# Weight products moved beside four waiting places of a two-block transformer kernel on one Trainium2 core

## The chip, the core and the metric

The program runs on one NeuronCore of one Trainium2 chip. The number that counts is the device time of one execution in microseconds (us). Three executions of the kernel before took 2319.35, 2320.1 and 2322.78 us, the median being 2320.1.

## The reference, cut to what matters

Two transformer blocks run one after the other over x of 512 tokens by 1024 features, in float32. The first has three attention branches and a feed-forward part; the change does not touch it. The second, which the change is about, computes:

```
h = rmsnorm_2(x, norm_mix)
qa, ka, va, za, alpha, beta, qb, kb, vb, ga, gb = _split_cols(h @ w_in, IN_SPLITS)
qa, ka, va = silu(_causal_dwconv(concat(qa, ka, va), conv_w))
g = -exp(a_log) * softplus(alpha + dt_bias); beta = sigmoid(beta); G = cumsum(g) in each chunk of 64
oa = _gated_deltanet(qa, ka, va, alpha, beta, a_log, dt_bias)       # 8 heads of 128
oa = rmsnorm_2(oa, head_norm) * silu(za)
ob = _chunk_band_attention(qb, kb, vb, band_bias)                   # 16 heads of 64, softmax
y = sigmoid(ga) * (oa @ w_a_out) + sigmoid(gb) * (ob @ w_b_out)
x = x + y @ w_o
q = rmsnorm_2(x, norm_xattn) @ w_mq;  kk, vv = split(rmsnorm_2(mem, norm_mem) @ w_mkv)
x = x + (softmax(q kk^T / 16) vv) @ w_mo                            # 4 heads of 256, 256 memory tokens
gate, up = split(rmsnorm_2(x, norm_ffn) @ w_gate_up)
x = x + (silu(gate) * up) @ w_down
```

## The kernel before

Everything is kept transposed, features on the 128 partitions and the 512 tokens along the free dimension. **A product** is 128 output columns of one weight matrix: eight weight blocks of 128x128 for an input of 1024 features. To reach float32 accuracy in the fast fp32r format each operand is split in a high and a low part, and each block takes three matmuls of 128x512: high by high (L1034), low by high (L1036), high by low (L1040). So a product is 24 matmuls. Key and value products of the memory (`mem_kv`) have 256 tokens and matmuls of 128x256. All small products (scores, sums, probabilities by v) go through `mm` at L989, all turnings (transposes by TensorE) through `tr` at L992.

**The weights** come in units of eight blocks (128x1024 float32, 512 KB), packed in the order in which the products use them. SyncE loads unit i+2 into one of three stage buffers (L2430), ScalarE copies unit i+1 to fp32r as whi (L1477), and VectorE (L1855) or GpSimd, here POOL (L2331), subtracts to get wlo. In the gated delta rule and the branch product behind it POOL does this, later VectorE. This step, `feed`, stands ahead of every eighth block in the order of work of all engines.

**The order of work** is written by class `Schedule`. Generators yield steps of one place in the program each; a step of a product is two blocks, six matmuls. `mix` alternates between generators, `par` merges them in proportion to their lengths, `pipe` chains products so that what follows one (a turning, say) stands some steps into the next, and an empty step (`repeat([], n)`) leaves n turns to the others. `settle` then makes one list, and every engine works through its part of it in that order and never passes a step that waits. It also gives each step its PSUM bank. Products alternate between b0 and b1 by a counter `gi`, which counts every product, and turnings marked "spare" take whichever of the two the counter says is free:

```
            if kind == "mm" and what[1] == 0:
                gi += 1
...
                if place == "gemm":
                    place = f"b{gi % 2}"
                elif place == "spare":
                    place = f"b{(gi if ended else gi + 1) % 2}"
```

A `Use` of a place carries in `freed` the events after which the next user may write to it; for a turning that is `act_turn`, ScalarE's copy out of the bank.

The four places that the change touches, in order of time:

1. `gdn_scalars` (L688) runs beside the first projections of the gated delta rule's first head (`mix` in `block2`). The product for alpha and beta, w_in_2 4096, is scaled by VectorE into tile ya; `gs_in` turns it (bank<-cft,ya), ScalarE and VectorE make g (tile al) and beta (tile be); `gs_cols` sums g in the chunks (bank<-al,cft), from which ScalarE takes gcol and VectorE ercol; `gs_rows` makes the same sums as rows (bank<-cft,al and cft,be). The rr in the scaling is the norm's factor, from the matmuls bank<-acc,cft.
2. `gated("a2")` (L589) is the branch oa @ w_a_out. Its first products begin in `opened` (L610): steps k0 to k5, which read the first six heads' output, before the last two heads are needed. oah and oal are the high and low part of the last head's output.
3. The band stage in `block2` (L802 on): `soft_pair` works through a couple of heads in four blocks of 128 queries (`sm_s` scores, `sm_max`, `sm_exp`, `sm_turn` the turning bank<-cft,bdp of the probabilities, copied by ScalarE to bdpt, `sm_pv` bank<-bdpt,bv). Beside couple p run the q, k and v products of couple p+1, and `raw_gate` products for the later branch as listed in `beside`. The v product (tile bvT) is turned (bank<-cft,bvT) and copied by ScalarE to bv (L1556); the o copies are obh.
4. `xattn`: after `mem_kv` with its 16 products, `cross(i, j)` works on memory head i in two halves, each with scores (bank<-mk,xq), exponential (xap, L1663), turning and the product with mv. The q products of head i+2 (`proj`) stand beside heads 0 and 1.

Of the kernel before, what the change touches and what calls it, by code (L numbers as in the profile page):

```python
# [293 lines left out]
def st(kind, what, *uses):  # L294
    return kind, what, uses
# [7 lines left out]
def mix(*parts):  # L303
    parts = list(parts)
    while parts:
        for p in list(parts):
            if (s := next(p, None)) is None:
                parts.remove(p)
            else:
                yield s  # L310
# [11 lines left out]
def par(*parts):  # L322
    parts = [list(p) for p in parts]
    done = [0] * len(parts)
    while any(n < len(p) for n, p in zip(done, parts)):
        i = min((i for i in range(len(parts)) if done[i] < len(parts[i])), key=lambda i: (done[i] + 0.5) / len(parts[i]))
        yield parts[i][done[i]]
        done[i] += 1
# [43 lines left out]
class Schedule:  # L372
# [15 lines left out]

    def raw_gate(self, name, col, out, ph):

        return self.gemm(name, col, range(8), ("H", ph), "h", None, [("dve_ev", (name, col, 0))], extra=[Use(f"raw{col}", [])], out=out)

    def gate(self, name, col, out, place, ph):
        return self.gemm(name, col, range(8), ("H", ph), "gate", place, [("dve_ev", (name, col, 0))], out=out)
# [194 lines left out]
    def gated(self, tag, ph, gates, branches, bufs, pre, late=False):  # L589
        n, mg = 0, {"b1": "mg1", "b2": "mg2"}.get(tag)  # L590
        if tag == "a2":
            yield from self.opened(tag, branches, bufs, pre)
        for m in range(2 if tag == "a2" else 0, 8):
            A = bufs[2 + m % 2]
            uA = Use(f"{tag}acc{m % 2}", [("gt_copy", m)] if tag == "a2" else [("sp_hi", (mg, m)), ("sp_lo", (mg, m))])
            for j, ((gname, gcol), (bname, src, nk)) in enumerate(zip(gates, branches)):
                gkey, bkey = (gname, gcol + 128 * m, 0), (bname, 128 * m, 0)
                s, t_ = pre.get((m, j), (bufs[n % 2], f"{tag}s{n % 2}"))[0], bufs[4 + n % 2]
                if late and (m, j) in pre:
                    yield [st("late_gate", (gkey, s))]  # L600
                if (m, j) not in pre:
                    yield from self.gate(gname, gcol + 128 * m, s, Use(f"{tag}s{n % 2}", [("dve_ev", bkey)]), ph)
                ut = Use(f"{tag}t{n % 2}", [("gt_add", (tag, m, j))])
                yield from self.gemm(bname, 128 * m, range(nk), src, "branch", uA if j == 0 else ut, [("dve_ev", bkey)],
                                     s=s, A=A, t=t_, j=j, tag=tag, m=m, s_key=gkey)
                n += 1
            ref = ("gt_add", (tag, m, len(gates) - 1)) if len(gates) > 1 else ("dve_ev", bkey)
            yield [st("merge", (tag, m, A, ref))]

    def opened(self, tag, branches, bufs, pre):  # L610

        (bname, src, nk), made = branches[0], []
        for m in range(2):
            A, bkey = bufs[2 + m], (bname, 128 * m, 0)
            g = self.gemm(bname, 128 * m, range(nk), src, "branch", Use(f"{tag}acc{m}", [("gt_copy", m)]), [("dve_ev", bkey)],
                          s=pre[m, 0][0], A=A, t=None, j=0, tag=tag, m=m, s_key=("w_in_2", 7184 + 128 * m, 0))
            made.append((g, [st("merge", (tag, m, A, ("dve_ev", bkey)))]))
        for g, _ in made:
            yield from islice(g, nk // 2 - 1)
        for g, merge in made:  # L620
            yield from g
            yield merge
# [64 lines left out]

    def gdn_scalars(self):  # L688
        u = Use("b5", [("gs_be", 0)])
        yield [st("gs_in", u, u)]  # L690
        yield from repeat([], 5)
        u = Use("b7", [("gs_er", 0)])
        yield [st("gs_cols", u, u)]
        ub, ub2 = Use("b7", [("gs_row", 0)]), Use("b6", [("gs_row", 1)])
        rows = [Use(f"gbc{h}", self.gbc_freed(h)) for h in range(2)]
        yield [st("gs_rows", (ub, ub2), ub, ub2)]
        yield from repeat([], 8)
        yield [st("gs_store", None)] + [st("gdn_rows", (h, rows[h]), rows[h]) for h in range(2)]
# [108 lines left out]
    def block2(self):  # L807
        k = self.k
        yield [st("lo_engine", "pool"), st("gdn_start", None)]
        yield from self.proj("w_in_2", 4096, k.goT, Use("goT", [("pe_small", "gdn")]), "mix2")  # L810
        yield from mix(self.gdn_scalars(), self.gdn_proj(0))
        pre = {}

        def pre_gates(i):
            bufs = [(f"g{n}{i}", k.g3[i][n]) for n in "qkv"] + ([("gz2", k.gz[2]), ("gz0", k.gz[0])] if i else [])
            for m, (place, b) in enumerate(bufs, 3 * i):
                pre[m, 0] = b[:], place
                yield from self.gate("w_in_2", 7184 + 128 * m, b[:], Use(place, []), "mix2")
        yield [st("none", None, *(Use(n, [("st_rows", 0)]) for n in ("gD", "gL")))]
        yield [self.decay(0, "chunk", ("gp_lt", 0))]  # L820
        for h in range(9):
            g = []
            if h >= 1:
                g.append(self.gdn_scan(h - 1))
            if h < 8:
                g.append(self.gdn_prep(h))
                g.append(self.gdn_proj(h + 1))
            if h >= 7:
                g.append(pre_gates(h - 7))
            yield from par(*g)  # L830
        yield [st("fence", "a2")]
        yield from self.gated("a2", "mix2", [("w_in_2", 7184)], [("w_a_out_2", "oa", 8)], k.a2buf, pre)
        yield [st("fence", "band"), st("lo_engine", "dve"), st("tables", None), st("load_mem", 2)]

        def proj(p):
            s, d = p % 2, self.done2("band", p)
            return [(self.proj("w_in_2", 4112 + 128 * p, k.bq[s][:], Use(f"bq{s}", d), "mix2", scale=0.125), None),
                    (self.proj("w_in_2", 5136 + 128 * p, k.bk[s][:], Use(f"bk{s}", d), "mix2"), None),
                    self.values("w_in_2", 6160 + 128 * p, "mix2", k.bvT, "bvT", k.bv[s], Use(f"bv{s}", d))]

        early = {}

        def gates(*ms):
            for m in ms:
                early[m, 0] = k.bgate[m][:], None
            return [(self.raw_gate("w_in_2", 8208 + 128 * m, k.bgate[m][:], "mix2"), None) for m in ms]
        beside = [[], [], [], gates(0), gates(1), gates(2), gates(3), gates(4, 5)]

        def band_loads(p):
            for h in (2 * p, 2 * p + 1):  # L850
                u = Use(f"band{h % 4}", [("sm_mx", (("band", h // 2, h % 2), 3))])
                yield [st("band_load", (h, u), u)]
        yield from band_loads(0)
        yield from pipe(proj(0))
        for p in range(8):
            if p < 7:
                yield from band_loads(p + 1)
            yield from par(self.soft_pair("band", p, "bd", "ob"), pipe((proj(p + 1) if p < 7 else []) + beside[p]))
        yield [st("fence", "mg2")]
        yield from self.gated("b2", "mix2", [("w_in_2", 8208)], [("w_b_out_2", "ob", 8)], k.b2buf, early, True)  # L860
        yield from self.residual("w_o_2", "mg2", range(8), "x2", "norm_xattn_2", ("w_in_2", 8208 + 896, 0))
        yield [st("fence", "xattn")]
# [25 lines left out]
    def xattn(self):  # L888
        k = self.k
        yield [st("tables", None)]  # L890

        def proj(i):
            for j in range(2):
                s = 2 * (i % 3) + j
                yield from self.proj("w_mq_2", 256 * i + 128 * j, k.xq[s][:], Use(f"xq{s}", [("pe_xo", (i, 1)), ("pe_xo", (i, 3))]), "x2")
        yield from par(seq(proj(0), proj(1)), self.mem_norm(2, "norm_mem_2"))
        yield from self.mem_kv(2, "w_mkv_2", k.raw2, 8, k.mk2, k.mv2, None, range(16))
        self.xo = [[Use(f"b{6 + j}", [("o_hi", ("o3", 2 * i + j)), ("o_lo", ("o3", 2 * i + j))]) for j in range(2)] for i in range(4)]
        for i in range(4):
            yield from par(self.cross(i, 0), self.cross(i, 1), *([proj(i + 2)] if i < 2 else []))  # L900
            yield [st("xa_out", i)]
        yield from self.residual("w_mo_2", "o3", range(8), "ffn", "norm_ffn_2", ("w_mq_2", 896, 0))
        yield [st("fence", "ff2")]
# [1677 lines left out]
```

How the kernel before makes its waits and increments, by code:

```python
    def free(use):  # L994
        for ref in use.before:
            if fresh(*ref):
                pe.wait_ge(*at(*ref))
# [1 line left out]
    def wait(*refs):  # L999
        for ref in refs:
            if fresh(*ref):
                pe.wait_ge(*at(*ref))
# [19 lines left out]
    def product(g, x):  # L1022
        o = bank[g.use.bank][:, 0:g.n]
        if x == 0:
            free(g.use)
        for j in (x, x + 1):
            unit, n = divmod(g.blocks[j], UNIT)
            c = slice(128 * n, 128 * n + 128)
            wh, wl = k.whi[unit % NSPLIT][:, c], k.wlo[unit % NSPLIT][:, c]
            hi, lo, hi_refs, lo_refs = moving(g, g.ks[j])
            if fresh("whi", unit):
                pe.wait_ge(*at("whi", unit))
            wait(*hi_refs)
            pe.matmul(o, wh, hi, start=j == 0, stop=False)
            wait(*lo_refs)
            pe.matmul(o, wh, lo, start=False, stop=False)
            if fresh(k.lo_sem[unit], unit):
                pe.wait_ge(*at(k.lo_sem[unit], unit))
            end = j == len(g.ks) - 1
            i = pe.matmul(o, wl, hi, start=False, stop=end)
            if end or n == UNIT - 1 or g.blocks[j] == len(k.blocks) - 1:
                i.then_inc(*up("pe_w", *([("unit", unit)] if n == UNIT - 1 else []), *([g.key] if end else [])))
# [1 line left out]
    def rms(ph, use):  # L1044
        if ph == "mix":
            pe.wait_ge(*at("ld_cf", 0))
        if ph == "fin":
            pe.wait_ge(*at("acc_add", (ph, 6)))
            free(use)
# [13 lines left out]
    def head_norm(o):  # L1063
        pe.wait_ge(*at("hn_sq", o.no))
        free(o.u_bank)
```

## Time and profile before

| | |
|---|---|
| median of three executions | 2320.1 us |
| their range | 2319.35 to 2322.78 us |
| the profiled execution, in all | 2320.8 us |
| its span, first to last instruction | 2319.0 us |
| TensorE (PE) busy, 13098 matmuls | 2254.3 us, 97% |
| TensorE weight loads (PEld) | 1798.2 us, 78% |
| VectorE (DVE) busy | 1141.5 us, 49% |
| ScalarE (ACT) busy | 892.9 us, 39% |
| GpSimd (POOL) busy | 443.7 us, 19% |
| mean DMA rate | 86 GB/s |

The page comes from one execution recorded by the hardware profiler. A row of the timeline gives start, duration, engine, line, operation, tiles (out<-in) and, in brackets, how long the engine had been idle and what ended that. The ends of matmuls are modelled and overlap the next start. Equal neighbours are drawn together in one row (x4). The granted clock is TensorE's, as a share of full speed.

### The profile page before, as it was taken

How to read it: one execution, taken by the hardware profiler on the slowest of the kernel's cores; microseconds unless marked ns; L12 is line 12 of the kernel's file. 1: busy time of each engine (PE TensorE's matmuls, PEld its weight loads, DVE VectorE, ACT ScalarE, POOL GpSimd, SP SyncE). 2: the span in 40 equal slices, each digit the busy share in tenths (PEclk: the TensorE clock that was granted, in tenths of full speed). 3: DMA queues.
4: the chain of work that ended last, by engine and by line, in shares of the span. 5: the costliest groups of instructions: out<-in, count | busy, mean ns of one | idle time of the engine just before them, and what ended most of it. 6: DMA issues, size and time to landing. Idle time of an engine off the chain costs nothing.

```text
span 2319.0 us, 32779 instructions
## 1 busy us (share of the span) xinstructions
PE 2254.3 (97%) x13098; PEld 1798.2 (78%) x13098; DVE 1141.5 (49%) x1949; ACT 892.9 (39%) x1427; POOL 443.7 (19%) x300
## 2 busy tenths in 40 slices
PE   8999999999999999999999999999999999999998
PEld 6776777888888888777777777777788988888886
DVE  4433454444544445575666512555546445435444
ACT  5544564233322223434443442444434434222223
POOL 2332221001201102444353332000011001101001
PEclk9999999999999999999999999999999999999999
DMA  4223212323333233221121123222232513233322
GB/s 166 73 64 101 64 46 82 100 92 99 93 98 101 92 99 92 95 71 47 47 70 51 38 66 128 81 82 83 63 100 92 155 37 100 91 100 100 98 93 82
DMA packets 58358, 198.95 MB, mean 86 GB/s; under 512 B 6736, under 2 KB 6864, under 8 KB 57952
## 3 DMA queue, kind: packets, MB, share of 16 engines
q1 hardware_dynamic: 58208, 196.86, 27.0%
q8 instruction: 105, 1.72, 0.3%
q14 instruction: 45, 0.37, 0.1%
HBM read 194.67 MB, written 2.16 MB: 85 GB/s over the span
## 4 chain that ended last, share of the span: by engine, by line
PE 87%; DVE 6%; ACT 3%; issue 2%; DMA 1%; POOL 0%; SPq 0%; DVEq 0%; ACTq 0%; POOLq 0%
PE bank L1034 24%; PE bank L1040 24%; PE bank L1036 24%; PE bank L989 13%; PE bank L992 2%; ACT whi L1477 1%; DMA stage<-in_wall 1%; DVE ya L1855 1%; DVE gk L1858 1%; DVE wlo L1855 0%; DVE gk L2130 0%; DVE sbA L2032 0%; SPq L2430 0%; DVE gq L1858 0%; DVE gv L1858 0%
## 5 line engine op out<-in xcount | busy, mean ns | idle before, releaser
L1034 PE MATMUL bank<-hh,whi 128*128 128x512 f32 x1680 | 688.0, 410 | 1.1 <-ACT nm1r L1517 0.6
L1040 PE MATMUL bank<-hh,wlo 128*128 128x512 f32 x1680 | 658.1, 392 | 4.8 <-DVE wlo L1855 3.1
L1036 PE MATMUL bank<-hl,whi 128*128 128x512 f32 x1680 | 656.0, 390 | 0.0
L1477 ACT ACTIVATE whi<-stage 128x1024 fp32r<-128x1024 f32 x340 | 357.3, 1051 | 326.5 <-PE bank L1040 315.5
L1855 DVE TENSOR_TENSOR wlo<-stage,whi 128x1024 fp32r<-128x1024 f32 x252 | 331.5, 1316 | 295.6 <-ACT whi L1477 295.1
L1040 PEld LDWEIGHTS bank<-hh,wlo 128*128 128x128 f32 x1680 | 315.9, 188 | 75.9 <-DVE wlo L1855 5.7
L1034 PEld LDWEIGHTS bank<-hh,whi 128*128 128x128 f32 x1680 | 316.5, 188 | 73.2 <-issue 9.3
L1036 PEld LDWEIGHTS bank<-hl,whi 128*128 128x128 f32 x1680 | 316.8, 189 | 63.6 <-issue 5.3
L2331 POOL TENSOR_TENSOR wlo<-stage,whi 128x1024 fp32r<-128x1024 f32 x88 | 210.6, 2393 | 408.1 <-ACT whi L1477 408.1
L1855 DVE TENSOR_TENSOR x<-bank,x 128x512 f32<-128x512 f32 x80 | 55.3, 691 | 152.6 <-PE bank L1040 152.6
L2331 POOL TENSOR_TENSOR acc<-acc,sqb 128x512 f32<-128x512 f32 x34 | 45.2, 1329 | 288.9 <-ACT sqb L1490 288.9
L1034 PE MATMUL bank<-u1h,whi 128*128 128x512 f32 x256 | 99.6, 389 | 0.0
L1036 PE MATMUL bank<-u1l,whi 128*128 128x512 f32 x256 | 99.6, 389 | 0.0
L1040 PE MATMUL bank<-u1h,wlo 128*128 128x512 f32 x256 | 99.6, 389 | 0.0
L2331 POOL TENSOR_TENSOR u1l<-f1t,u1h 128x512 fp32r<-128x512 f32 x32 | 41.3, 1292 | 265.2 <-ACT u1h L1575 265.2
L2331 POOL TENSOR_TENSOR u2l<-f2s,u2h 128x512 fp32r<-128x512 f32 x22 | 28.4, 1293 | 299.7 <-ACT u2h L1584 299.7
L989 PEld LDWEIGHTS bank<-ya 64*64 64x64 f32 (+1 forms) x2048 | 58.9, 138 | 32.2 <-issue 16.5
L989 PE MATMUL bank<-ya 64*64 64x64 f32 (+2 forms) x2048 | 72.4, 231 | 5.9 <-DVE ya L1855 5.8
L1575 ACT ACTIVATE u1h<-f1t 128x512 fp32r<-128x512 f32 x32 | 20.2, 632 | 126.6 <-DVE f1t L1855 126.6
L1036 PE MATMUL bank<-u2l,whi 128*128 128x512 f32 x176 | 68.6, 390 | 0.0
L1034 PE MATMUL bank<-u2h,whi 128*128 128x512 f32 x176 | 68.5, 389 | 0.0
L1040 PE MATMUL bank<-u2h,wlo 128*128 128x512 f32 x176 | 68.5, 389 | 0.0
(374 smaller groups left out, 3446.4 us busy)
## 6 DMA issues: line engine op xcount, KB each, us to landing
stage<-in_wall SPq DMA_DIRECT2D x340, 512.0 KB, 3.6
band<-in_toep SPq DMA_DIRECT2D x16, 256.0 KB, 3.9
x<-in_xT SPq DMA_DIRECT2D x8, 256.0 KB, 5.2
fb<-rowsf SPq DMA_DIRECT2D x8, 256.0 KB, 3.7
gbc<-rows SPq DMA_DIRECT2D x8, 256.0 KB, 3.3
gbc<-rowsc SPq DMA_DIRECT2D x16, 128.0 KB, 3.6
out_y<-fout SPq DMA_DIRECT2D x8, 256.0 KB, 2.3
memx<-in_memT SPq DMA_DIRECT2D x1, 1024.0 KB, 10.0
```

The source lines that it names most:

```text
L989: return pe.matmul(out, w, r, start=start, stop=stop, skip_group_check=True)
L992: return pe.transpose(out, in_, k.cf("ident"))
L1034: pe.matmul(o, wh, hi, start=j == 0, stop=False)
L1036: pe.matmul(o, wh, lo, start=False, stop=False)
L1040: i = pe.matmul(o, wl, hi, start=False, stop=end)
L1477: act.activation(k.whi[u % NSPLIT][:], k.stage[u % NSTAGE][:], ACT.Copy).then_inc(*up("whi", u))
L1575: act.activation(k.u1[0][:, a["t"] % 16, :], a["b"][:], ACT.Copy).then_inc(*up("sp_hi", ("u1", a["t"])))
L1855: return dve.tensor_tensor(out, a, b, op)
L1858: return dve.scalar_tensor_tensor(out=out, in0=a, scalar=s, in1=b, op0=op0, op1=op1)
L2331: return pool.tensor_tensor(out, a, b, op)
```

## The change

It does four things. `gdn_scalars` lets three steps of others go by before `gs_in`. `opened` begins four products, each in a bank of its own from b2 to b5, instead of two, and the loop of `gated` goes on at the fifth. In the band stage the raw gates are in bank b7 and run as one stream, three steps beside each of couples 0 to 6 and the rest, nine, beside couple 7; before, they stood whole beside couples 3 to 6 with two beside 7. In `xattn` the last four key and value products stand beside cross attention's head 0, and the q products of heads 2 and 3 move on to stand beside heads 1 and 2; head 3 has none.

```diff
--- before.py
+++ after.py
@@ -388,7 +388,8 @@
 
     def raw_gate(self, name, col, out, ph):
 
-        return self.gemm(name, col, range(8), ("H", ph), "h", None, [("dve_ev", (name, col, 0))], extra=[Use(f"raw{col}", [])], out=out)
+        return self.gemm(name, col, range(8), ("H", ph), "h", None, [("dve_ev", (name, col, 0))], extra=[Use(f"raw{col}", [])],
+                         bank="b7", out=out)
 
     def gate(self, name, col, out, place, ph):
         return self.gemm(name, col, range(8), ("H", ph), "gate", place, [("dve_ev", (name, col, 0))], out=out)
@@ -590,7 +591,7 @@
         n, mg = 0, {"b1": "mg1", "b2": "mg2"}.get(tag)
         if tag == "a2":
             yield from self.opened(tag, branches, bufs, pre)
-        for m in range(2 if tag == "a2" else 0, 8):
+        for m in range(4 if tag == "a2" else 0, 8):
             A = bufs[2 + m % 2]
             uA = Use(f"{tag}acc{m % 2}", [("gt_copy", m)] if tag == "a2" else [("sp_hi", (mg, m)), ("sp_lo", (mg, m))])
             for j, ((gname, gcol), (bname, src, nk)) in enumerate(zip(gates, branches)):
@@ -610,10 +611,10 @@
     def opened(self, tag, branches, bufs, pre):
 
         (bname, src, nk), made = branches[0], []
-        for m in range(2):
-            A, bkey = bufs[2 + m], (bname, 128 * m, 0)
-            g = self.gemm(bname, 128 * m, range(nk), src, "branch", Use(f"{tag}acc{m}", [("gt_copy", m)]), [("dve_ev", bkey)],
-                          s=pre[m, 0][0], A=A, t=None, j=0, tag=tag, m=m, s_key=("w_in_2", 7184 + 128 * m, 0))
+        for m in range(4):
+            A, bkey = bufs[2 + m % 2], (bname, 128 * m, 0)
+            g = self.gemm(bname, 128 * m, range(nk), src, "branch", Use(f"{tag}acc{m % 2}", [("gt_copy", m)]), [("dve_ev", bkey)],
+                          bank=f"b{2 + m}", s=pre[m, 0][0], A=A, t=None, j=0, tag=tag, m=m, s_key=("w_in_2", 7184 + 128 * m, 0))
             made.append((g, [st("merge", (tag, m, A, ("dve_ev", bkey)))]))
         for g, _ in made:
             yield from islice(g, nk // 2 - 1)
@@ -687,6 +688,7 @@
 
     def gdn_scalars(self):
         u = Use("b5", [("gs_be", 0)])
+        yield from repeat([], 3)
         yield [st("gs_in", u, u)]
         yield from repeat([], 5)
         u = Use("b7", [("gs_er", 0)])
@@ -840,11 +842,12 @@
 
         early = {}
 
-        def gates(*ms):
-            for m in ms:
+        def gates():
+            for m in range(6):
                 early[m, 0] = k.bgate[m][:], None
-            return [(self.raw_gate("w_in_2", 8208 + 128 * m, k.bgate[m][:], "mix2"), None) for m in ms]
-        beside = [[], [], [], gates(0), gates(1), gates(2), gates(3), gates(4, 5)]
+                yield from self.raw_gate("w_in_2", 8208 + 128 * m, k.bgate[m][:], "mix2")
+        slow = gates()
+        beside = [[(islice(slow, 3), None)] for _ in range(7)] + [[(slow, None)]]
 
         def band_loads(p):
             for h in (2 * p, 2 * p + 1):
@@ -894,10 +897,11 @@
                 s = 2 * (i % 3) + j
                 yield from self.proj("w_mq_2", 256 * i + 128 * j, k.xq[s][:], Use(f"xq{s}", [("pe_xo", (i, 1)), ("pe_xo", (i, 3))]), "x2")
         yield from par(seq(proj(0), proj(1)), self.mem_norm(2, "norm_mem_2"))
-        yield from self.mem_kv(2, "w_mkv_2", k.raw2, 8, k.mk2, k.mv2, None, range(16))
+        yield from self.mem_kv(2, "w_mkv_2", k.raw2, 8, k.mk2, k.mv2, None, range(12))
+        beside = [self.mem_kv(2, "w_mkv_2", k.raw2, 8, k.mk2, k.mv2, None, range(12, 16)), proj(2), proj(3), []]
         self.xo = [[Use(f"b{6 + j}", [("o_hi", ("o3", 2 * i + j)), ("o_lo", ("o3", 2 * i + j))]) for j in range(2)] for i in range(4)]
         for i in range(4):
-            yield from par(self.cross(i, 0), self.cross(i, 1), *([proj(i + 2)] if i < 2 else []))
+            yield from par(self.cross(i, 0), self.cross(i, 1), beside[i])
             yield [st("xa_out", i)]
         yield from self.residual("w_mo_2", "o3", range(8), "ffn", "norm_ffn_2", ("w_mq_2", 896, 0))
         yield [st("fence", "ff2")]
```

The matmuls are the same 13098. In the changed kernel the lines 1034, 1036, 1040, 989 and 992 are 1038, 1040, 1044, 993 and 996.

**TensorE at the turning of `gdn_scalars`.** The names: hh and hl are the input's two parts, acc the sum of squares of the norm, cft a constant tile. Before:

```order
L989 MATMUL bank<-acc,cft 128x512 [waits r_ln,acc_add]
L989 MATMUL bank<-cft,ya 128x16 [waits dve_ev]
L989 MATMUL bank<-cft,ya 128x16 x3
L1034 MATMUL bank<-hh,whi 128x512 [waits whi]
L1036 MATMUL bank<-hl,whi 128x512
L1040 MATMUL bank<-hh,wlo 128x512 [waits wlo_pool]
```

After:

```order
L993 MATMUL bank<-acc,cft 128x512 [waits r_ln,acc_add]
L1038 MATMUL bank<-hh,whi 128x512 [waits whi,dve_ev]
L1040 MATMUL bank<-hl,whi 128x512
L1044 MATMUL bank<-hh,wlo 128x512 [waits wlo_pool]
L1038 MATMUL bank<-hh,whi 128x512
L1040 MATMUL bank<-hl,whi 128x512
```

Twelve matmuls of the next product, w_in_2 1024, now stand ahead of the turning and twelve behind it. Further on, the sums by columns and by rows had six matmuls between them; now they are neighbours:

```order
L993 MATMUL bank<-al,cft 128x32 [waits r_ln,dve_small]
L993 MATMUL bank<-al,cft 128x32
L993 MATMUL bank<-al,cft 64x32 x2
L993 MATMUL bank<-cft,al 8x128 [waits dve_small]
L993 MATMUL bank<-cft,al 8x128 x3
```

The six matmuls went ahead of the columns' sums.

**TensorE at the end of couple 0 of the band stage, with the banks' numbers.** Before:

```order
L989 MATMUL bank6<-bdpt1,bv0 64x128
L992 MATMUL bank0<-cft,bvT 128x128 [waits dve_ev]
L992 MATMUL bank0<-cft,bvT 128x128 x3
L1034 MATMUL bank1<-hh,whi0 128x512 [waits whi]
L1036 MATMUL bank1<-hl,whi0 128x512
```

After:

```order
L1038 MATMUL bank7<-hh,whi0 128x512
L1040 MATMUL bank7<-hl,whi0 128x512
L1044 MATMUL bank7<-hh,wlo0 128x512
L996 MATMUL bank0<-cft,bvT 128x128 [waits dve_ev]
L996 MATMUL bank0<-cft,bvT 128x128 x3
L1038 MATMUL bank0<-hh,whi0 128x512 [waits act_turn]
L1040 MATMUL bank0<-hl,whi0 128x512
```

A step of a raw gate in bank 7 now stands ahead of the turning of v, and the q product behind it writes the bank of the turning, where it wrote the other one. The same pair of rows, turning and next product in one bank, stands at the ends of couples 0, 1, 2, 3 and 5.

## Rows read from the trace of the kernel before

**Rows 1.** The page: busy time of TensorE; the weights' low part on VectorE.
```profile
PE 2254.3 (97%) x13098; PEld 1798.2 (78%) x13098; DVE 1141.5 (49%) x1949; ACT 892.9 (39%) x1427; POOL 443.7 (19%) x300
...
L1855 DVE TENSOR_TENSOR wlo<-stage,whi 128x1024 fp32r<-128x1024 f32 x252 | 331.5, 1316 | 295.6 <-ACT whi L1477 295.1
```

**Rows 2.** TensorE's waits over the whole span: us in total, times, longest us.
```profile
PE bank L989 <- ACT xap L1663: 3.0, 2, 1.5
...
PE bank L989 <- ACT bdpt L1637: 2.7, 3, 0.9
...
PE bank L992 <- DVE bdp L2032: 0.2, 1, 0.2
```

**Rows 3.** Timeline of TensorE, place 1: start, us, engine, line, operation [idle <- releaser].
```profile
937.91 1.02 PE L989 MATMUL bank<-acc,cft 128*128 128x512 f32 x2
941.16 1.06 PE L989 MATMUL bank<-cft,ya 16*128 16x16 f32 x8 [2.22 <-DVE ya L1858]
942.15 0.60 PE L1034 MATMUL bank<-hh,whi 128*128 128x512 f32 x1
...
945.90 0.39 PE L1034 MATMUL bank<-hh,whi 128*128 128x512 f32 x1
...
947.98 0.76 PE L989 MATMUL bank<-al,cft 128*128 128x32 f32 x8
948.68 0.50 PE L1034 MATMUL bank<-hh,whi 128*128 128x512 f32 x1
...
950.26 1.26 PE L989 MATMUL bank<-cft,al 128*8 128x128 f32 x10
...
952.98 0.50 PE L1034 MATMUL bank<-hh,whi 128*128 128x512 f32 x1
```

**Rows 4.** Windows of 1 us, place 1; the clock stands ahead of the DMA share.
```profile
943.00:944.00 1.00, 1.00 (x4) 0.81 (x3) 0.43 (x3) 0.56 (x3) 0.00 (x0) 0.50 0.01 4
```

**Rows 5.** Timeline of POOL, place 1.
```profile
937.45 2.35 POOL L2331 TENSOR_TENSOR wlo<-stage,whi 128x1024 fp32r<-128x1024 f32 x1 [1.39 <-ACT whi L1477]
```

**Rows 6.** Timeline of VectorE, place 1.
```profile
949.11 0.19 DVE L1855 TENSOR_TENSOR ercol<-bank,gcol 128x32 f32<-128x32 f32 x1 [4.32 <-ACT gcol L1700]
```

**Rows 7.** Timeline of TensorE, place 2.
```profile
1385.18 0.50 PE L1034 MATMUL bank<-oah,whi 128*128 128x512 f32 x1 [0.93 <-ACT whi L1477]
...
1387.70 0.50 PE L1040 MATMUL bank<-oah,wlo 128*128 128x512 f32 x1 [1.79 <-POOL wlo L2331]
```

**Rows 8.** Timeline of ScalarE, place 2.
```profile
1384.09 1.99 ACT L1477 ACTIVATE whi<-stage 128x1024 fp32r<-128x1024 f32 x2
```

**Rows 9.** Timeline of POOL, place 2.
```profile
1382.32 1.28 POOL L2331 TENSOR_TENSOR oal<-ya,oah 128x512 fp32r<-128x512 f32 x1 [0.74 <-ACT oah L1747]
```

**Rows 10.** Timeline of TensorE, place 3, couple 0 and couple 3.
```profile
1467.93 1.10 PE L992 MATMUL bank<-cft,bdp 128*128 128x128 f32 x8
1469.92 1.09 PE L989 MATMUL bank<-bdpt,bv 128*64 128x128 f32 x16 [0.89 <-ACT bdpt L1637]
1470.94 0.66 PE L992 MATMUL bank<-cft,bvT 128*128 128x128 f32 x4
1471.35 0.47 PE L1034 MATMUL bank<-hh,whi 128*128 128x512 f32 x1
...
1553.42 0.60 PE L992 MATMUL bank<-cft,bvT 128*128 128x128 f32 x4
```

**Rows 11.** Timeline of ScalarE, place 3, couple 0 and couple 3.
```profile
1468.69 1.08 ACT L1637 ACTIVATE bdpt<-bank 128x512 f32<-128x512 f32 x2 [3.54 <-PE bank L992]
...
1554.06 0.60 ACT L1556 ACTIVATE bv<-bank 128x512 f32<-128x512 f32 x1 [1.17 <-PE bank L992]
```

**Rows 12.** Timeline of TensorE, place 4, heads 1 and 2 of cross attention.
```profile
1862.81 0.48 PE L1034 MATMUL bank<-hh,whi 128*128 128x512 f32 x1
...
1881.81 1.89 PE L989 MATMUL bank<-mk,xq 128*128 128x256 f32 x8
...
1892.08 1.25 PE L989 MATMUL bank<-mk,xq 128*128 128x256 f32 x5
```

## The prediction, made before the changed kernel had run

> **What bounds the kernel now.** I read the busy line of the page first. TensorE is busy 97% of 2319.0 us, and the next engine, VectorE, 49% [rows 1]. A change that only puts the same matmuls in another order can win no more than the time in which TensorE waits or runs at its lower clock, so I went to TensorE's own waits next. Of those at the four places, the exponential of cross attention costs 3.0 us in two waits, the copy of the turned band probabilities 2.7 in three, and the band probabilities themselves 0.2 in one [rows 2]. Then I read the timeline of TensorE in each place, and the engines it waits for.
>
> The reader should see one more thing there. A listed matmul of 128x512 lasts 0.39, but the next starts after a good half of that: nine of them lie between 945.90 and 947.98 [rows 3], so one costs 0.231 and a step (six, two weight blocks) 1.39. The first matmul behind small work is listed at 0.50 instead (948.68), so I give such a restart 0.1. All terms below are from start to start. The Trainium skill (Perfetto Trace Analysis, section Identifying the Most-Contended Engine) warns that matmul busy time is a bad measure, because matmuls are pipelined; by it the 97% is no proof that only 3% can be won.
>
> **Place 1, the turning in the gated delta rule's scalars.** Before, TensorE issues the two norm matmuls at 937.91 and the turning at 941.16, after 2.22 idle for VectorE's ya; then the product at 942.15, whose first nine matmuls take 3.75 up to 945.90 where nine at full pace take 2.08 [rows 3]. The granted clock there is 0.50, the 1.2 GHz level [rows 4], and it fell right after that idle. The norm pair is passed at 938.77 (its 1.02, less the 0.16 by which a listed matmul overlaps the next). To the next product at 952.98 this place costs 14.2.
> After, twelve product matmuls stand first: 0.1 + 2.77. Their third needs POOL's wlo, done at 937.45 + 2.35 = 939.80 [rows 5], while TensorE gets there at 938.77 + 0.1 + 0.46 = 939.33: a new wait of 0.53 with the hand-over. The turning starts near 942.2, after ya's end at about 941.1, so it waits for nothing: 0.99. Twelve more: 2.87. Then the columns' sums, 0.70 (947.98 to 948.68), and directly behind them the rows' sums, which before had a product step between. They read ercol, which ended 1.32 after the columns' start (949.11 + 0.19 against 947.98) [rows 3, 6]: 1.32 - 0.70, with a hand-over 0.65. The rows' sums take 2.72 (950.26 to 952.98). Sum 2.87 + 0.53 + 0.99 + 2.87 + 0.70 + 0.65 + 2.72 = 11.3. **Term 1: -2.9.** Bounds: -1.3 if the half-clock stretch stays (1.6 comes back), -4.0 if both new waits vanish.
>
> **Place 2, four products begun instead of two.** TensorE waits 0.93 for ScalarE's whi and 1.79 for POOL's wlo, at 1385.18 and 1387.70 [rows 7]. What they wait for is not the head's output but a weight unit: ScalarE splits two units from 1384.09 [rows 8], late, because that split is queued behind the last head's sigmoid work. The head's last output, oal, is ready at 1382.32 + 1.28 = 1383.60 [rows 9], and even with two products begun TensorE needs it only in the second unit, after the wait. The change puts other blocks of the same branch into these units, but the unit's boundary and the place of its split on ScalarE and POOL stay. **Term 2: 0.** Bounds: -2.7 if both waits go; +0.5 if the later merges are late.
>
> **Place 3, raw gates beside every couple of band heads.** Three things.
> (a) A step between the last turning of the probabilities and the last product with v hides ScalarE's copy. Before, couples 0, 1 and 2 have none, which is the 2.7 in three [rows 2]; the pattern is 1467.93 to 1469.92 with 0.89 idle [rows 10]. After, couples 1 and 6 have none: **-0.9**.
> (b) The gates now name bank b7, yet each still counts in the alternation of b0 and b1. At the ends of couples 0, 1, 2, 3 and 5 the turning of v and the q product behind it thus get the same bank (second pair of fences above): the product's first matmul may start only when ScalarE has copied the turned values out. Before, the two were in different banks and the product started 0.41 after the turning (1470.94 to 1471.35) [rows 10]. The price: from the turning's start to the copy's 0.64 (1553.42 to 1554.06), the copy 0.60, copy to TensorE 0.15 (copies end at 1468.69 + 1.08, TensorE goes on at 1469.92), less 0.41 = 0.98 [rows 10, 11]. Five times: **+4.9**. No row of before shows this hand-over itself; the bounds are 0 (the copy lies in the shade of something) and 2.0 each (a whi of 1.0 ahead of the copy on ScalarE [rows 8]). I take the middle, since ScalarE's order puts the copy right behind the o copies, a product step earlier, and the next whi behind it.
> (c) In couple 7 a weight split, 1.0 on ScalarE [rows 8] and 1.3 on VectorE [rows 1], comes to stand ahead of an exponential that has a step of 1.39 as cover: +0.9; the 0.2 for bdp [rows 2] goes. Runs of products are broken by small work six times more: +0.6.
> **Term 3: -0.9 + 4.9 + 0.9 - 0.2 + 0.6 = +5.3.**
> The Trainium skill (Perfetto Trace Analysis, section Matmuls) speaks against this edit: independent matmul groups should rotate through different PSUM banks, so that the evacuation of one overlaps the next. By it (b) is a cost, as I forecast; without (b) term 3 would be +0.4.
>
> **Place 4, key and value products beside cross attention.** Heads 0 and 1 stand beside q products, 2 and 3 are bare. From head 1's first product matmul at 1862.81 to 1881.81 are 19.0, less 48 matmuls at 0.231 (11.1) and with the restarts counted as the head's: 7.9. Bare head 2 takes 1881.81 to 1892.08 = 10.3 [rows 12], so covering one saves 2.4, and after it only head 3 is bare: -2.4. But head 0 now stands beside products over 256 columns, whose steps are half as long, 0.7 for 1.39. At two of its turnings the split pair [rows 1, 8] stands ahead of the exponential, and 2 x 0.7 = +1.4 of cover is missing; more switches, +0.3. **Term 4: -0.7**, bounds -2.4 and +1.
>
> **The sum**: -2.9 + 0 + 5.3 - 0.7 = +1.7. The profiled execution took 2320.8 in all with a span of 2319.0, 0.7 above the median of the three runs, 2320.1; I set the change against the median: **2321.8 us**. SyncE's loads keep their places against the splits, so I give them nothing. About 0.2%, 4.6 us, is what a measurement of this kernel can tell from no change, so "same" is 2315.5 to 2324.7.
>
> **Rivals.**
> Forecast, 0.50: as summed, 2319.5 to 2324.
> The hand-overs don't show, 0.20: ScalarE is only 39% busy and the product's weights could be loading meanwhile. Against: TensorE's order is fixed, and a matmul cannot pass the one that waits. 1.7 - 4.9 = -3.2, 2316.9.
> All four do what their place suggests, 0.06: -2.9, -2.7, all three holes of place 3 gone (-2.7) and -2.4 make -10.7, 2309.4. Against: place 2's waits are a weight unit's, and two holes stay.
> **Slower**, 0.13: at the ends of the five couples a whi of 1.0 gets ahead of the copy in time, because the o copies wait behind it. Each hand-over then costs 2.0, 5.0 more in all: 2326.8. It decides once the copy starts over 1.6 after the turning, where 0.64 is forecast.
> The clock, 0.11: TensorE's clock fell to 1.2 GHz after the wait of 2.22 [rows 3, 4]; behind the wait of 1.79 the matmul is listed at 0.50, as at any restart at full clock [rows 7]. If two of the five new hand-overs bring such a stretch at 1.6, +3.2: 2325.0. The Trainium skill (TensorE: Matmul & The Clock Gate, section A second HAM failure mode: psum-queue depth-cycling) describes just this, short idles between groups that cycle through banks and set off the lower clock again and again; the rows here show no drop behind the wait of 1.79.
>
> **How the numbers follow.** Faster than 2315.5: the third case and a quarter of the second, 0.11. Slower than 2324.7: the fourth case, half of the fifth and a tail of the first, 0.21. The rest, 0.68, is the same. The range runs from the second case, with term 1 at its better end, 2315.5, to just under the fourth, 2326.5.
>
> **What would show it.** Right: at 938 to 953 no 2.22 wait and no window at 0.50, and a wait of about 0.5 for POOL's wlo and of 0.6 for ercol; the two waits near 1385 nearly as they are; in the band stage five waits of a product for ScalarE's bv copy, 0.8 to 1.0 each, and two for bdpt; one wait of 1.5 for xap instead of two, and small ones in head 0. Wrong: no wait for bv, which leads to the second case; waits over 1.6 for it, to the fourth; waits at 1385 gone, to the third; a half-clock stretch in the band stage, to the fifth.

## The result, and the profile after

The changed kernel took 2327.48 us in the median of eight runs (2326.46 to 2329.81), the kernel before, run beside it and earlier, 2322.28 (2319.35 to 2324.26, eight runs). The ratio is 1.0027, with a 95% interval of 1.0017 to 1.0036: 6.3 us slower (3.9 to 8.4); the two medians themselves lie 5.2 apart. The forecast was +1.7, 2321.8, with a range up to 2326.5. The direction of the likeliest case was right and its size far too small: 2327.48 lies 1.0 above the range. Some of that is the yardstick, since the kernel before came out 2.2 above the median that the forecast was counted from. The profiled execution's span went from 2319.0 to 2326.6.

The page of the changed kernel:

```profile
span 2326.6 us, 32763 instructions
...
PE 2257.8 (97%) x13098; PEld 1799.1 (77%) x13098; DVE 1141.4 (49%) x1949; ACT 894.2 (38%) x1427; POOL 444.5 (19%) x300
```

TensorE has the same 13098 matmuls and is busy 3.5 more in all, against [rows 1], so some of the 7.6 is a slower clock and the rest waits. TensorE's waits (us in total, times, longest):

```profile
PE bank L1044 <- POOL wlo L2335: 4.2, 4, 1.8
...
PE bank L1038 <- ACT bv L1560: 3.4, 5, 0.7
PE bank L996 <- DVE bdp L2036: 3.4, 3, 1.8
...
PE bank L993 <- ACT bdpt L1641: 1.8, 2, 0.9
PE bank L993 <- ACT xap L1667: 1.5, 1, 1.5
...
PE bank L1038 <- ACT whi L1481: 1.4, 2, 0.9
...
PE bank L996 <- DVE xap L2073: 0.8, 1, 0.8
...
PE bank L993 <- DVE ercol L1859: 0.6, 1, 0.6
```

Against [rows 2], xap went from 3.0 in two waits to 1.5 in one, with a new 0.8 for VectorE's part of the probabilities, and bdpt from 2.7 to 1.8. The wait of 2.22 for ya [rows 3] is gone. New are bv, 3.4 in five, as forecast (listed at 0.69 each, 0.8 to 1.0 were expected), and **bdp, 3.4 in three, where before had 0.2 in one and I had forecast that it goes**.

**Place 1.** The timeline of TensorE:

```profile
938.40 1.02 PE L993 MATMUL bank<-acc,cft 128*128 128x512 f32 x2
...
940.34 0.50 PE L1044 MATMUL bank<-hh,wlo 128*128 128x512 f32 x1 [0.46 <-POOL wlo L2335]
...
942.82 1.06 PE L993 MATMUL bank<-cft,ya 16*128 16x16 f32 x8
...
946.66 0.76 PE L993 MATMUL bank<-al,cft 128*128 128x32 f32 x8
948.04 1.26 PE L993 MATMUL bank<-cft,al 128*8 128x128 f32 x10 [0.61 <-DVE ercol L1859]
...
950.75 0.50 PE L1038 MATMUL bank<-hh,whi 128*128 128x512 f32 x1
```

From the norm matmuls to the next product are 12.35 instead of 15.07 [rows 3]: -2.7. The two small waits stand where they were expected (0.46 and 0.61), and no window there shows the lower clock; only the product's first matmul, right behind the norm matmuls, is listed longer than the rest, at 0.80.

**Place 2.** TensorE, and the granted clock in a window behind the waits (the figure ahead of the DMA share):

```profile
1381.62 0.50 PE L1038 MATMUL bank<-oah,whi 128*128 128x512 f32 x1 [0.92 <-ACT whi L1481]
...
1384.14 0.80 PE L1044 MATMUL bank<-oah,wlo 128*128 128x512 f32 x1 [1.79 <-POOL wlo L2335]
1384.74 0.63 PE L1038 MATMUL bank<-oah,whi 128*128 128x512 f32 x1
...
1385.00:1386.00 1.00, 1.00 (x3) 0.73 (x3) 0.00 (x0) 0.00 (x0) 1.00 (x1) 0.50 0.70 82
```

The waits are those of [rows 7], 0.92 and 1.79. But behind them the clock is at 0.50 (1.2 GHz) for almost six microseconds, which it was not in before. Twelve matmuls at 0.427 instead of 0.227, with the first of the stretch and the one behind it, cost 2.8.

**Place 3.** At the end of couple 0, TensorE and ScalarE:

```profile
1473.51 0.60 PE L996 MATMUL bank<-cft,bvT 128*128 128x128 f32 x4
1474.80 0.50 PE L1038 MATMUL bank<-hh,whi 128*128 128x512 f32 x1 [0.69 <-ACT bv L1560]
...
1474.14 0.60 ACT L1560 ACTIVATE bv<-bank 128x512 f32<-128x512 f32 x1 [0.82 <-PE bank L996]
```

The product stands 1.29 behind the start of the turning instead of 0.41 [rows 10]. ScalarE's copy starts 0.63 after the turning and takes 0.60, as worked out. Then couples 2, 3 and 4, at the last turning of the probabilities:

```profile
1531.99 1.25 PE L996 MATMUL bank<-cft,bdp 128*128 128x128 f32 x8 [1.84 <-DVE bdp L2036]
...
1563.98 1.25 PE L996 MATMUL bank<-cft,bdp 128*128 128x128 f32 x8 [0.64 <-DVE bdp L2036]
...
1596.28 1.25 PE L996 MATMUL bank<-cft,bdp 128*128 128x128 f32 x8 [0.89 <-DVE bdp L2036]
```

and what VectorE and ScalarE do ahead of the first of them:

```profile
1527.81 1.23 DVE L1859 TENSOR_TENSOR wlo<-stage,whi 128x1024 fp32r<-128x1024 f32 x1 [5.05 <-ACT whi L1481]
1528.96 0.68 DVE L2025 CUSTOM_DVE_ANT_0 bdzb<-bank,band 128x512 f32<-128x512 f32 x1
...
1530.65 0.69 DVE L1862 SCALAR_TENSOR_TENSOR bvT<-bank,rr 128x512 f32<-128x512 f32 x1
...
1531.44 0.49 DVE L2036 TENSOR_SCALAR bdp<-bdp,bdst 128x512 f32<-128x512 f32 x1
...
1526.72 1.06 ACT L1481 ACTIVATE whi<-stage 128x1024 fp32r<-128x1024 f32 x1 [0.83 <-PE bank L1044]
1529.93 0.72 ACT L1634 ACTIVATE bdp<-bdzb,bdst 128x512 f32<-128x512 f32 x1 [2.15 <-DVE bdst L2028]
```

The reader should see the order: ScalarE's split (whi, 1526.72), VectorE's (wlo, to 1529.0), only then the maximum (bdzb, 1528.96), then the exponential (1529.93), then the scaling by VectorE (1531.44, and again for the other head), and TensorE, which has nothing left but a small product, waits 1.84. VectorE's eviction of v's product (bvT, 1530.65) stands ahead of the scaling too. In couple 3 that eviction alone makes the wait. No split falls there, and both exponentials were done by 1561.9, but VectorE first waits for v's last matmul, evicts it, and only then scales:

```profile
1562.64 0.69 DVE L1862 SCALAR_TENSOR_TENSOR bvT<-bank,rr 128x512 f32<-128x512 f32 x1 [2.29 <-PE bank L1044]
...
1563.44 0.49 DVE L2036 TENSOR_SCALAR bdp<-bdp,bdst 128x512 f32<-128x512 f32 x1
```

Before, at the end of couple 2, the scaling came first and v's eviction behind it:

```profile
1518.88 0.49 DVE L2032 TENSOR_SCALAR bdp<-bdp,bdst 128x512 f32<-128x512 f32 x1
1520.81 0.69 DVE L1858 SCALAR_TENSOR_TENSOR bvT<-bank,rr 128x512 f32<-128x512 f32 x1 [1.44 <-PE bank L1040]
```

Behind the wait of 1.84 too the clock fell:

```profile
1534.00:1535.00 1.00, 1.00 (x4) 0.66 (x2) 0.00 (x0) 0.00 (x0) 0.03 (x1) 0.50 0.83 332
```

From the first turning of v in this stage to the first matmul of the branch product behind it, before took 227.1 and the changed kernel 236.5: +9.4 instead of the +5.3 forecast.

**Place 4.** From the last matmul of that branch product to the first of the cross attention's output product are 176.1 before and 174.9 after: -1.2.

### The profile page after: what moved, and what is told of

The parts are those of the page before. It is cut to its first block, busy times and chain, and to the rows that moved or that the text cites. A ratio compares the mean times of both kernels' runs of the same rounds, so it can differ in the third digit from the quotient of the medians.

```text
span 2326.6 us, 32763 instructions
## 1 busy us (share of the span) xinstructions
PE 2257.8 (97%) x13098; PEld 1799.1 (77%) x13098; DVE 1141.4 (49%) x1949; ACT 894.2 (38%) x1427; POOL 444.5 (19%) x300
## 4 chain that ended last, share of the span: by engine, by line
PE 51%; DVE 4%; ACT 2%; issue 2%; POOL 0%; DMA 0%; DVEq 0%; SPq 0%; ACTq 0%; POOLq 0%
PE bank L1038 14%; PE bank L1044 13%; PE bank L1040 13%; PE bank L993 9%; PE bank L996 2%; ACT whi L1481 1%; DVE ya L1859 1%; DVE gk L1862 0%; DVE wlo L1859 0%; DVE gk L2134 0%; DMA stage<-in_wall 0%; DVE gq L1862 0%; DVE gv L1862 0%; POOL wlo L2335 0%; DVE cuu L1859 0%
```

## The experiments

All were run in five rounds beside the kernel before; each ratio is to it, with its 95% interval. A ratio of 1.001 is 2.3 us.

**The four places, each alone in the kernel before.** The edits are the diff's own parts: `repeat([], 3)` in `gdn_scalars` (place 1); `opened` and its loop (place 2); `raw_gate`, `gates` and `beside` of the band stage (place 3); `mem_kv` and `beside` in `xattn` (place 4).

e1_place1. 

> The kernel before with place 1 alone (three steps ahead of gs_in). Theory T (each place acts by itself, as the trace of the changed kernel reads): the wait of 2.2 for ya goes, two waits of about 0.5 and 0.6 come, 12.3 to 12.4 from the norm matmuls to the next product where before took 15.1; time -2.7 against before. Rival R (clock): the time won is lost again, because TensorE's clock falls to 1.2 GHz somewhere later, as it did in the changed kernel near 1383; then the waits of 0.9 and 1.8 at the start of the a2 branch are followed by a window at 0.50 here too, though place 2 is untouched, and the gain is near 0 to -1.

Measured: 0.9987 (0.9979 to 0.9996), -3.0. The theory holds, and the gain isn't lost again. In this run's trace the waits of 0.9 and 1.8 at place 2 are there, and the clock stays full behind them.

e2_place2. 

> The kernel before with place 2 alone (four products begun, banks b2 to b5). Theory T: the two waits of 0.93 and 1.79 stay, and so does the time, within 0.5 of before, since the half-clock stretch that the changed kernel shows there is not made by the order of the products. Rival R: four products in four banks bring the half-clock stretch themselves: a window at 0.50 right behind the waits, +3.0.

Measured: 1.0000 (0.9991 to 1.0009). Four products begun instead of two change nothing that can be measured, in either direction, and no window near 1385 shows a lower clock. The traces of e3, e4, e5, e9, e11 and e12 do show one there, and in all six place 2 is as before. So the change at place 2 isn't what brings the half-clock stretch.

e3_place3. 

> The kernel before with place 3 alone (raw gates in b7, three steps a couple). Theory T: five waits of the q product for ScalarE's bv copy, 0.93 each from start to start (+4.7), three waits of the last turning of the probabilities for VectorE's bdp in couples 2, 3 and 4, 1.9, 0.7 and 1.0 (+3.6), one hole for bdpt fewer (-1.0): +7 without a half-clock stretch, +8.5 with one. My forecast, rival here: the bdp waits don't belong to this edit but come from the shift by the other places; then +5.3.

Measured: 1.0038 (1.0024 to 1.0051), +8.8. The waits of TensorE are those of the changed kernel:

```profile
PE bank L1036 <- ACT bv L1558: 3.4, 5, 0.7
PE bank L994 <- DVE bdp L2034: 3.4, 3, 1.8
...
PE bank L991 <- ACT bdpt L1639: 1.8, 2, 0.9
```

The bdp waits belong to this edit, and this edit alone costs more than the whole change.

e4_place4. 

> The kernel before with place 4 alone (four key and value products beside head 0 of cross attention). Theory T: one wait of 1.5 for xap instead of two, one of 0.8 for the xap probabilities in head 0: -1.2. Rival: narrow products are too short a cover, two waits of over 0.7 in head 0, and -0.2 to +0.5.

Measured: 0.9994 (0.9985 to 1.0002), -1.4 with an interval that touches zero. In the trace one wait of 1.5 for xap went and one of 0.8 came, which fits.

The four sum to -3.0 + 0 + 8.8 - 1.4 = +4.4, inside the interval of the whole, 3.9 to 8.4.

**Is it the bank?** e5_banks keeps place 3's order and takes the products in b7 out of the alternation:

```diff
-            if kind == "mm" and what[1] == 0:
+            named = kind in ("mm", "ev") and (what[0] if kind == "mm" else what).use.place == "b7"
+            if kind == "mm" and what[1] == 0 and not named:
                 gi += 1
-            if kind in ("mm", "ev"):
+            if kind in ("mm", "ev") and not named:
                 ended = kind == "ev"
```

> Place 3 alone as in e3_place3, in the same order, but the products in b7 no longer count in the alternation of b0 and b1, so the turning of v and the q product behind it are in different banks again. Theory T (the hand-over of the bank costs 0.93 each): the five waits for bv are gone, the bdp waits stay, and the time falls by 4.7 against e3_place3, to about +4.1 against before. Rival R: TensorE would have waited there anyhow, for the weights or ScalarE's split that stand behind the copy; the waits only change their name, and the time stays at +7 to +9.

Measured: 1.0020 (1.0011 to 1.0030), +4.6, so 4.2 less than e3_place3 (the two ran at different times, each against its own runs of before). No wait for bv is left, and those for bdp are unchanged:

```profile
PE bank L995 <- DVE bdp L2035: 3.4, 3, 1.8
...
1475.99 0.60 PE L995 MATMUL bank<-cft,bvT 128*128 128x128 f32 x4
1476.35 0.48 PE L1037 MATMUL bank<-hh,whi 128*128 128x512 f32 x1
```

The product starts 0.36 behind the turning, where the changed kernel had 1.29: 0.93 a time, 4.7 for five. The time fell by about that, so the waits didn't only change their name. The traces agree: from the first turning of v to the branch product are 236.34 in e3_place3 and 230.25 here. Of these 6.1, 4.7 are the hand-overs; the rest is a half-clock stretch in couple 2 that e3_place3's trace has and this one hasn't.

e7_b7_only is the other half of the question: the bank alone, nothing moved.

```diff
         return self.gemm(name, col, range(8), ("H", ph), "h", None, [("dve_ev", (name, col, 0))], extra=[Use(f"raw{col}", [])],
-                         out=out)
+                         bank="b7", out=out)
```

> The kernel before with the raw gates in bank b7 and nothing moved. Theory T: the bank as such costs nothing; the cost comes when turning and next product are neighbours in one bank, and here a gate step stands between: 0, no wait for bv. Rival R: b7 itself costs, through its other users (the norm's factors): +0.5 or more.

Measured: 1.0005 (0.9996 to 1.0014), and no wait for bv in the trace. Naming a bank costs nothing that can be measured, though the rival's +0.5 isn't excluded: one wait of 0.8 for bgate came, where the two gates beside couple 7 follow each other in b7, and the stage is 0.4 longer. What costs is that the turning and the next product become neighbours in one.

**Where do the bdp waits come from?** e6_front is e5_banks with the gate steps ahead of the couple's products:

```diff
-pipe((proj(p + 1) if p < 7 else []) + beside[p])
+pipe(beside[p] + (proj(p + 1) if p < 7 else []))
```

> e5_banks with one more edit: the three gate steps stand ahead of the couple's q, k and v products instead of behind them, so that in the last block of each couple one product step stands between the maximum and the exponential again, and one between exponential and turning. Theory T (the bdp waits come from the one product step that is missing there, and from the weight split in couples 2 and 4): no bdp wait, no bdpt wait either, since a step of v's product covers the copy in every couple, and -4 against e5_banks, which is 0 to -2.5 against before. Rival R: the waits come from what else the stream of gates brings (evictions on VectorE, splits), and at least 2 of the 3.6 remain.

Measured: 1.0021 (1.0012 to 1.0030), +4.9: nothing won against e5_banks. A miss, and the waits say why:

```profile
PE bank L995 <- DVE bvT L1861: 3.1, 3, 1.2
...
PE bank L1037 <- DVE bgate L1861: 2.7, 3, 1.8
...
PE bank L995 <- DVE bdp L2035: 1.3, 4, 0.4
```

The bdpt waits are gone and bdp is down from 3.4 to 1.3, so the missing step was a cause. In couple 3 there is no wait for bdp at all now. The four that are left stand in couples 2 and 4, two of 0.43 and 0.22 in each, where the weight split is ahead of the maximum. But gates now follow each other directly in the one bank b7, and the next may begin only when VectorE has evicted the last (bgate, 2.7 in three, 1.83 the longest). And where a weight split stands just ahead of the last step of v's product, its eviction is late for the turning (two waits of 1.18). The waits moved.

e12_lo_pool tells the two causes of the bdp waits apart by taking VectorE's share of the split away from e5_banks:

```diff
-        yield [st("fence", "band"), st("lo_engine", "dve"), st("tables", None), st("load_mem", 2)]
+        yield [st("fence", "band"), st("tables", None), st("load_mem", 2)]
...
-        yield [st("fence", "mg2")]
+        yield [st("fence", "mg2"), st("lo_engine", "dve")]
```

> e5_banks with the weights' low part made by POOL in the band stage, so that the subtraction of 1.23 no longer stands on VectorE ahead of the maximum. Theory T (in couples 2 and 4 it is the weight split in the chain that makes TensorE wait for bdp, in couple 3 the missing product step): of the waits 1.84, 0.64 and 0.89 the first falls by about 1.2 to 0.6, the last to 0, the middle one stays; -2 against e5_banks unless POOL's slower subtraction, 2.4, makes TensorE wait for wlo. Rival R: the evictions of the gates on VectorE make the wait, and all three stay within 0.3.

TensorE at the last turnings of couples 2 and 3 in its trace, and its waits:

```profile
1537.93 1.25 PE L995 MATMUL bank<-cft,bdp 128*128 128x128 f32 x8 [0.43 <-DVE bdp L2035]
...
1567.54 1.25 PE L995 MATMUL bank<-cft,bdp 128*128 128x128 f32 x8 [0.64 <-DVE bdp L2035]
...
PE bank L1043 <- POOL wlo L2334: 9.3, 4, 5.5
...
PE bank L995 <- DVE bdp L2035: 5.1, 6, 1.4
```

At the three turnings the waits are now 0.43, 0.64 and none, where they were 1.84, 0.64 and 0.89. That bears the theory out, and the first fell a little further than the 0.6 expected: in couples 2 and 4 it was the split in the chain, in couple 3 the product step that stood elsewhere. What is left in couple 2 has a reason of its own, which the same trace shows:

```profile
1535.21 2.39 POOL L2334 TENSOR_TENSOR wlo<-stage,whi 128x1024 fp32r<-128x1024 f32 x1 [7.39 <-ACT whi L1480]
...
1536.24 1.64 DVE L2035 TENSOR_SCALAR bdp<-bdp,bdst 128x512 f32<-128x512 f32 x1
```

VectorE's scaling took 1.64 instead of 0.49 while POOL subtracted. The kernel as a whole is slower, 1.0054 (1.0041 to 1.0067), +12.5. The same slow scalings, up to 2.55, bring bdp waits in other blocks, up to 1.4. And TensorE waits 5.5 once for POOL's wlo at the entry of the stage: ScalarE had finished the whi at 1429.9, but POOL's subtraction stands behind two memsets of the tile band, which waited for their DMA, and starts at 1435.18. From 1435 to 1441 the clock is at 0.50.

**A version that keeps what works.** e8_joined puts places 1 and 4 together with e6_front.

> Places 1 and 4 as in the change, place 2 as before, place 3 as in e6_front. Theory T: the terms add, -3.0 - 1.3 and 0 to -2.5: -4.3 to -6.8 against before. Rival R (clock): waits that go bring a half-clock stretch elsewhere, which gives back 1.7 to 3: -2 to -4.

Measured: 1.0006 (0.9997 to 1.0015), +1.4, worse than theory and rival. The reason is e6_front's, whose own +4.9 was not known when this was written: -3.0 - 1.4 + 4.9 = +0.5, which the interval covers. The trace of this run also has a half-clock stretch in the band stage (near 1538, behind the bgate wait of 1.83) that e6_front's lacks, as the rival had it; whether that is in the other executions isn't known.

e9_places14 is the change without places 2 and 3.

> The kernel before with places 1 and 4 of the change, places 2 and 3 left as they were. Theory T: the two terms add, -3.0 and -1.3, so -4.3 against before, and no wait for bv. Rival R: they don't add, because the half-clock stretches shift with the work ahead of them: between 0 and -2.

Measured: 0.9986 (0.9977 to 0.9995), -3.2, somewhat under the sum of -4.4 and within both intervals.

e10_tail goes after the three bdpt waits with another edit, without the gates. In `soft_pair`:

```diff
-        yield []
+        yield from repeat([], 3 if kind == "band" and p < 3 else 1)
         yield [st("sm_pv", (two, 3, use))]
```

The last two steps of v's product then stand between the last turning and the last product with v.

> The kernel before with one edit of its own: in band couples 0 to 2, where nothing hides the copy of the turned probabilities, three steps instead of one are left free ahead of the last product with v, so that the last two steps of v's product come to stand there. Theory T: the three bdpt waits of 0.9 go, nothing takes their place, -2.9. Rival R: the step that hid the maximum and exponential of the last block is gone from there, and bdp waits of 0.6 or more each come in their stead: -1 to 0.

Measured: 0.9994 (0.9985 to 1.0003), -1.4 with an interval that takes in zero and the theory's -2.9, so the time doesn't decide. The rival's new bdp waits didn't come. In the trace bdpt is gone from the waits, and of bdp the old 0.2 is left in the table:

```profile
PE bank L992 <- DVE bdp L2032: 0.2, 1, 0.2
```

By the trace alone the stage is 1.7 shorter (225.4 from the first turning of v to the branch, 227.1 before). Less than the 2.9 of the theory: three waits of 0.89 went, and what took the place of the rest was not followed.

e11_joined2 is e9_places14 with that edit.

> e9_places14 with the edit of e10_tail. Theory T: the sum of the two, -7 if both theories hold. Rival R: as in those two.

Measured: 2316.34 us against 2321.38, 0.9979 (0.9970 to 0.9988): **4.9 us faster than the kernel before**, and faster than the changed one. The -7 of the theory is at the edge of the interval; -3.2 and -1.4, as measured alone, sum to -4.6. Its waits at the four places:

```profile
PE bank L1042 <- POOL wlo L2333: 4.2, 4, 1.8
...
PE bank L991 <- ACT xap L1665: 1.5, 1, 1.5
...
PE bank L994 <- DVE xap L2071: 0.8, 1, 0.8
...
PE bank L991 <- DVE ercol L1857: 0.6, 1, 0.6
...
PE bank L994 <- DVE bdp L2034: 0.2, 1, 0.2
```

## Why the prediction was wrong

**Term 1, -2.9: right.** The trace shows -2.7, the run of it alone -3.0. Both new waits came at their places: from start to start, less the work between, 0.62 for 0.53 and 0.68 for 0.65 (listed 0.46 and 0.61).

**Term 2, 0: right.** e2_place2 is at 1.0000. The waits are a weight unit's and stayed. The half-clock stretch there in the changed kernel is told of below; it isn't this edit's.

**Term 3, +5.3: here the prediction failed**, by 3.5 in e3_place3 (+8.8) and by 4.1 in the trace.
- (a) the holes for bdpt, -0.9: right, three became two.
- (b) the bank hand-over, 0.98 each: right. Measured 0.93 five times against e5_banks, +4.7, and shown by that run; against the 0.41 of before, from which the 0.98 was counted, it is 0.88. The rule of the Trainium skill (Perfetto Trace Analysis, section Matmuls) that independent groups should rotate through the banks agrees with the trace here, with these numbers. The rival that the hand-overs don't show falls, and so does the slower rival: the copy started 0.63 after the turning at couple 0, nowhere near 1.6, and no bv wait is longer than 0.7. The time came out near that rival's 2326.8, by another mechanism.
- (c) is **the step that failed: "the 0.2 for bdp goes", and a split ahead of an exponential only in couple 7, +0.9**. I had followed the steps between the last turning and the last product with v in every couple, but the steps between scores, maximum, exponential and last turning in couple 7 alone. With three gate steps put in, q, k and v's products are pushed earlier, the last block of couples 0 to 6 has both its v steps ahead of the maximum, and of what hides the chain of maximum, exponential and scaling one gate step is left, in couple 3 none: there one of the three steps is the gate's eviction, which gives TensorE nothing to do. VectorE's eviction of v's product has moved in between, directly ahead of the scaling; before it stood behind the turning in couples 0 to 2 and had two gate steps behind it in couple 3. In the changed kernel's couple 3 this eviction is what TensorE waits for. Where a weight split falls into this chain (couples 2 and 4), its whi and wlo are added. That cost 1.9, 0.7 and 1.0 from start to start, +3.6. e12_lo_pool and e6_front separate the two causes. In couple 7, where I had looked, there was no wait at all: the 0.9 did not come.
- The sum of what was measured: -0.9 + 4.7 + 3.6 - 0.4 (the old bdp wait, start to start) = +7.0. The remaining 2.4 of the trace's 9.4 are the half-clock stretch behind the wait of 1.84 and the switches, and e5_banks, which has the same wait without the stretch, tells them apart: from that turning to the turning of v behind it are 5.09 there and 6.64 in the changed kernel, so the stretch cost 1.55. That leaves some 0.8 for the switches, where 0.6 was forecast.

**Term 4, -0.7: the sign right**, -1.2 in the trace and -1.4 alone. The lack of cover in head 0 cost 0.8 instead of 1.4.

**The clock.** The rival with the half-clock stretch did occur, at couple 2, but behind a wait I hadn't foreseen, not behind the hand-overs of 0.69. Against the forecast's +1.7 the trace has: place 3's bdp waits and what hangs on them +4.1, and the stretch at place 2, +2.8, less one that before had near 1010 and this execution had not, -1.6. With +0.2 at place 1 and -0.5 at place 4 that makes 6.7 of the span's 7.6; 0.5 more had gathered ahead of place 1.

What the list of rivals lacked was the split in the softmax chain of couples 2 and 4, and v's eviction ahead of the scaling. The split's parts, 1.0 and 1.3, were in the rows.

## What to carry to other kernels

When steps are inserted into an order of work, count for every repetition what stands in each dependent chain, not only in the gap that the edit is meant to fill: a step that fills one gap is taken out of another. Periodic work that rides in the same queues (here a weight split every eight blocks, 2.3 us over two engines) falls elsewhere in every repetition, and in two of the three repetitions that waited here it was in the chain. Look also at what the edit puts ahead of the chain on the engine that works it off, such as an eviction ahead of the scaling here. And where a result is turned in a bank that the very next product writes, the copy out of that bank stands in the open, 0.93 a time here; giving some products a bank of their own is only half done while they still count in the others' alternation.

## What the runs showed of the hardware

The lower clock is not a property of a wait's length alone. The waits of 0.9 and 1.8 at place 2 are the same in all fourteen traces here, to a tenth. In seven of them (the changed kernel, e3, e4, e5, e9, e11, e12) the windows behind them show 0.50; in the other seven (before, e1, e2, e6, e7, e8, e10) they don't, and those seven, and only those, show a stretch at 0.50 near 1010, in work that is the same in all fourteen. Each of the fourteen had exactly one of the two. Behind the wait of 1.84 in couple 2 the clock fell in the changed kernel and in e3_place3, but not in e5_banks, which has the same wait; behind a wait of 1.83 for bgate it fell in e8_joined and not in e6_front. The stretch near 1010 cost 1.6; the one at place 2 cost 1.6 in e3, e4, e5, e9 and e12 and 2.8 to 2.9 in the changed kernel and e11. There is one trace of each kernel, so no two executions of the same kernel can be compared. But in before, e3, e4, e5, e6, e7, e10 and e12 all the work up to place 2 is the same, and they split four to four. So a difference of two traces has to be cleared of these stretches before it is put down to an edit. What selects between them stays open.

In e12_lo_pool VectorE's scaling of the probabilities stood nearly still while POOL subtracted: each of the 19 scalings listed above 0.5 us ran into one of POOL's subtractions, and none that ran clear of them took more than 0.49. The eviction of v's product (bvT) beside the subtraction at 1535.21 took its usual 0.69.

The listed idle time understates a stall: 0.69 listed was 0.93 from start to start at the hand-over, 1.79 was 1.96 at place 2.
